# Normed tokens as two fp32r parts in place of three bf16 parts, experts chosen tile by tile, four expert tiles in the residual's memory

## The reference

```
hf = rmsnorm(x, norm_ffn_g)                      # 256 tokens, width 1024
logits = hf @ w_router + b_router                # 32 experts
top_vals, top_idx = lax.top_k(logits, 4)
gates = softmax(top_vals)
for each expert e, for the tokens that chose it:
    gu = hf @ w1[e] + b1[e]                      # 1024 x 2048, float32
    act = (clip(up) + 1) * gate * sigmoid(1.702 * gate)
    y = act @ w2[e] + b2[e]                      # 1024 x 1024, float32
x = x + sum over the chosen experts of gates * y
return rmsnorm(x, norm_final_g)
```

## Time and profile before

| | us |
|---|---|
| median of 3 runs | 1248.23 |
| the profiled execution's own time | 1249.09 |
| its span in the profile | 1247.3 |
| TensorE busy | 1172.6 |
| TensorE weight loads busy | 593.5 |
| VectorE busy | 377.3 |
| ScalarE busy | 228.9 |
| GpSimd busy | 57.7 |

### The profile page before, as it was taken

The page is one execution under the profiler, slowest core; times in us unless marked ns, Lnnn a source line. Parts: engine busy times, 40 slices in busy tenths (PEclk is TensorE's granted clock), DMA queues, the critical chain, the costliest instruction groups (busy, mean ns, idle before and its releaser), DMA issues.

```text
span 1247.3 us, 17264 instructions
## 1 busy us (share of the span) xinstructions
PE 1172.6 (94%) x7208; PEld 593.5 (48%) x7208; DVE 377.3 (30%) x677; ACT 228.9 (18%) x342; POOL 57.7 (5%) x39
## 2 busy tenths in 40 slices
PE   8999999999999999999989999999999998998996
PEld 8999888888633333333333333333333333333332
DVE  5754765656522112121111122111121111111112
ACT  5444543544510001000000010000000000000001
POOL 0950000000300000000000000000000000000000
PEclk9999999999999999999999999999999999999999
DMA  9755435947899999999999999999999999999995
GB/s 309 265 202 175 164 135 202 355 152 283 360 428 428 427 428 428 428 429 428 428 428 429 428 427 428 429 428 429 429 428 428 429 428 428 428 429 429 428 428 220
DMA packets 56212, 461.88 MB, mean 370 GB/s; under 512 B 5617, under 2 KB 7346, under 8 KB 31634
## 3 DMA queue, kind: packets, MB, share of 16 engines
q1 hardware_dynamic: 52664, 457.99, 88.6%
q10 hardware_dynamic: 3514, 3.40, 0.9%
HBM read 460.30 MB, written 1.07 MB: 370 GB/s over the span
## 4 chain that ended last, share of the span: by engine, by line
PE 57%; DMA 39%; DVE 1%; ACT 1%; issue 1%; SPq 0%; DVEq 0%; ACTq 0%
DMA w_ring<-in_w 17%; PE ps L1207 15%; DMA behind_xb<-in_w 14%; PE ps L1257 11%; DMA behind_watt<-in_w 7%; PE ps L942 3%; PE ps L943 3%; PE ps L944 3%; PE ps L1301 3%; PE ps L1185 2%; PE ps L935 2%; PE ps L938 2%; PE ps L937 2%; PE ps L954 1%; PE ps L1080 1%; PE ps L1082 1%
## 5 line engine op out<-in xcount | busy, mean ns | idle before, releaser
L1207 PE MATMUL ps<-w_ring,A_W 128*64 128x512 f32 x1232 | 278.6, 597 | 33.3 <-DMA w_ring<-in_w 33.0
L1207 PEld LDWEIGHTS ps<-w_ring,A_W 128*64 128x64 f32 x1232 | 84.4, 136 | 204.5 <-issue 142.2
L1713 DVE TENSOR_SCALAR A_W<-ps 128x512 f32<-128x512 f32 x32 | 22.1, 692 | 499.3 <-PE ps L1207 499.3
L1257 PE MATMUL ps<-w_ring,A_W 128*64 128x512 f32 x624 | 141.4, 595 | 0.0
L1380 DVE TENSOR_TENSOR w_parts<-w_ring,w_parts 128x1024 fp32r<-128x1024 f32 x76 | 105.7, 1403 | 84.2 <-ACT w_parts L654 84.2
L850 ACT ACTIVATE A_W<-A_W 128x512 f32<-128x512 f32 x32 | 20.2, 630 | 526.1 <-DVE A_W L1713 526.1
L1207 PE MATMUL ps<-A_QK,A_W 128*64 128x512 f32 x416 | 94.8, 597 | 10.9 <-DMA A_QK<-in_w 10.9
L654 ACT ACTIVATE w_parts<-w_ring 128x1024 fp32r<-128x1024 f32 x76 | 80.1, 1059 | 75.7 <-PE ps L944 37.7
L1257 PEld LDWEIGHTS ps<-w_ring,A_W 128*64 128x64 f32 x624 | 42.5, 136 | 72.1 <-issue 70.5
L854 ACT ACTIVATE A_W<-ps 128x512 f32<-128x512 f32 x32 | 19.1, 598 | 299.8 <-PE ps L1238 299.8
L942 PE MATMUL ps<-w_parts,hT_hi 128*128 128x512 f32 x176 | 69.4, 394 | 0.0
(11 more groups left out here) (246 smaller groups left out, 1285.0 us busy)
## 6 DMA issues: line engine op xcount, KB each, us to landing
w_ring<-in_w SPq DMA_DIRECT2D x115, 2048.0 KB, 43.7
A_QK<-in_w SPq DMA_DIRECT2D x38, 2048.0 KB, 42.8
behind_watt<-in_w SPq DMA_DIRECT2D x19, 2048.0 KB, 43.7
behind_xb<-in_w SPq DMA_DIRECT2D x19, 2048.0 KB, 43.7
w_ring<-in_w_in SPq DMA_DIRECT2D x36, 1024.0 KB, 7.3
w_ring<-in_w_ret_branch SPq DMA_DIRECT2D x2, 2048.0 KB, 11.8
A_W<-in_w_out SPq DMA_DIRECT2D x1, 2560.0 KB, 14.3
xb<-in_x SPq DMA_DIRECT2D x4, 512.0 KB, 3.8
```

The costliest lines, as they stand in the source:

```text
L1207: mm = pe.matmul(o, XT[:, k, :], tile[:, j, c * HALF:(c + 1) * HALF], start=(k == 0), stop=(k == KC - 1))
L1257: mm = pe.matmul(ps[CAP * c:CAP * c + CAP, 3, :], lhs, w2_tile(flat)[:, q % W2_ROWS, c * HALF:(c + 1) * HALF], start=False, stop=(q == FQ ...
```

## The change

The normed tokens become two fp32r parts: `xs_hi`, which ScalarE rounds (`high_part`), and `xs_lo`, the rest, which VectorE subtracts (`low_part`, in the place of `first_rest`). The steps of the second and third bf16 part go away on ScalarE (8 instructions) and GpSimd (4). [...] A gather is 8 x 2 x 2 = 32 matmuls in place of 48.

VectorE chooses the experts of tile 0 and tile 1 one after the other (`choose_experts`), with one half of the low parts of tile 1 between them and the other half behind the selection. TensorE starts the logits of tile 1 when half of the transposes are stored, with 8 fewer fills ahead and 20 in place of 30 behind. ScalarE copies the first gathered tokens ahead of the gates' exponentials. Four tiles of the experts (`sg`, `act_sb`, `actT`, `y_sb`) move from 2048:4096 of `A_W`, where `xs_lo` now lies, to 6144:8192, the residual's place, so their first writers wait until the residual is in PSUM (`s_res`).

```diff
+        xs_lo = nc.alloc_sbuf_tensor_at("xs_lo", [P, TT, D], F32R, offset=nc.sbuf_base - 4 * 8192 + 4 * 2048)
+        s_one = nc.alloc_sbuf_tensor_at("s_one", [P, TT, CAP], F32R, offset=nc.sbuf_base - 4 * 8192 + 4 * 5632)
-        xs = nc.alloc_sbuf_tensor_at("xs", [P, 3, TT, D], BF16, offset=nc.sbuf_base - 4 * 2304)
+        xs_hi = nc.alloc_sbuf_tensor_at("xs_hi", [P, TT, D], F32R, offset=nc.sbuf_base - 4 * 2304)
...
-            second_rest(0, 0, 0)
-            second_rest(1, 0, 1)
-            second_rest(2, 1, 0)
-            second_rest(3, 1, 1)
             pool.wait_ge(s_lo, 2 * TT)
             pool.memset(sc_w, 0.0).then_inc(main.swe, 1)
+            pool.wait_ge(s_res, TT)
             pool.memset(y_sb, 0.0).then_inc(main.ye, 1)
...
-            middle_part(0)
             root(1)
             high_part(2)
             high_part(3)
-            middle_part(1)
-            middle_part(2)
-            middle_part(3)
-            for n in range(4):
-                low_part(n)
+            act.wait_ge(main.gathered, 1)
+            act.activation(XT.rearrange("p k s -> p (k s)"), bank(2), ACT.Copy).then_inc(main.x, 1)
             act.wait_ge(s_tk, 1)
...
-            fill(1, 8)
+            pe.wait_ge(s_xte, 3)
+            logits(1, range(4))
             pe.wait_ge(s_xte, 4)
-            logits(1, range(KC)).then_inc(s_lg, 1)
-            fill(2, 30)
+            logits(1, range(4, KC)).then_inc(s_lg, 1)
+            fill(2, 20)
...
                 for k in range(KC):
-                    for part in range(3):
+                    for part in range(2):
                         for t in range(TT):
-                            mm = pe.matmul(ps[:, 2, k * CAP:(k + 1) * CAP], xs[:, part, t, k * P:(k + 1) * P],
-                                           s_one[:, t, :], start=(part == 0 and t == 0), stop=(part == 2 and t == 1))
+                            mm = pe.matmul(ps[:, 2, k * CAP:(k + 1) * CAP], (xs_hi, xs_lo)[part][:, t, k * P:(k + 1) * P],
+                                           s_one[:, t, :], start=(part == 0 and t == 0), stop=(part == 1 and t == 1))
...
+            def choose_experts(t):
                 dve.wait_ge(s_lg, t + 1)
+                link(dve.scalar_tensor_tensor(lg[t], ps[:, t, 0:N_EXP], rstd[:, t:t + 1], br_sb[:, :], ALU.mult, ALU.add))
+                link(dve.max(best[:, t, :], lg[t]))
+                link(dve.max_index(ids[:, t, :].bitcast(U32), best[:, t, :], lg[t]))
...
+            choose_experts(0)
+            low_part(2)
+            choose_experts(1)
...
             slots(main, 0, 0)
+            low_part(3)
+            dve.wait_ge(s_lo, 2 * TT)
...
             dve.wait_ge(s_used, W1_UNITS)
+            dve.wait_ge(s_res, TT)
             activate(main, 0)
```

More of the change, by code:

```diff
@@ L200, in hybrid_block_kernel @@
         xg = A_W[:, 0:2048].rearrange("p (t d) -> p t d", t=TT)
-        rest = A_W[:, 2048:4096].rearrange("p (t d) -> p t d", t=TT)
         x2 = A_W[:, 6144:8192].rearrange("p (t d) -> p t d", t=TT)
-        chosen = A_W[:, 4096:4096 + TT * TOP_K * N_EXP].rearrange("p (t j e) -> p t j e", t=TT, j=TOP_K)
+        chosen = A_W[:, 5888:5888 + TT * TOP_K * N_EXP].rearrange("p (t j e) -> p t j e", t=TT, j=TOP_K)
         weighed = A_W[:, 4352:4352 + TT * TOP_K * N_EXP].rearrange("p (t j e) -> p t j e", t=TT, j=TOP_K)
@@ L226, in hybrid_block_kernel @@
         ul = A_W[:, 1536:2048]
[L227 to L230, removed]
+        sg = A_W[:, 6144:6656]
+        act_sb = A_W[:, 6656:7168]
+        actT = A_W[:, 7168:7680]
+        y_sb = A_W[:, 7680:8192]
         bias = bias_sb[0:BIAS_ROWS, :]
@@ L795, in high_part @@
                 act.wait_ge(s_r2, t + 1)
[L796 to L806, removed]
+                act.activation(xs_hi[:, t, cols], xg[:, t, cols], ACT.Copy, scale=rstd[:, t:t + 1]).then_inc(s_hi, 1)
             def root(t):
@@ L836, in _ @@
                                accum_out=gden[:, t:t + 1]).then_inc(s_tke, 1)
-            act.wait_ge(main.gathered, 1)
-            act.activation(XT.rearrange("p k s -> p (k s)"), bank(2), ACT.Copy).then_inc(main.x, 1)
             for t in range(TT):
@@ L1191, in gather_first @@
                 pe.wait_ge(main.slots, 1)
-                for part, ready in enumerate((s_hi, s_mid, s_lo)):
+                for part, ready in enumerate((s_hi, s_lo)):
                     pe.wait_ge(ready, 2 * TT)
@@ L1195, in gather_first @@
                         for t in range(TT):
-                            mm = pe.matmul(ps[:, 2, k * CAP:(k + 1) * CAP], xs[:, part, t, k * P:(k + 1) * P],
+                            mm = pe.matmul(ps[:, 2, k * CAP:(k + 1) * CAP], (xs_hi, xs_lo)[part][:, t, k * P:(k + 1) * P],
                                            s_one[:, t, :], start=(part == 0 and k == 0 and t == 0),
-                                           stop=(part == 2 and t == 1), skip_group_check=True)
+                                           stop=(part == 1 and t == 1), skip_group_check=True)
                 mm.then_inc(main.gathered, 1)
@@ L1600, in residual_scale, with low_part @@
                 dve.wait_ge(s_r2, t + 1)
-            def first_rest(n):
+            def low_part(n):
                 t, h, cols = HALVES[n]
                 dve.wait_ge(s_hi, n + 1)
-                dve.scalar_tensor_tensor(rest[:, t, cols], xg[:, t, cols], rstd[:, t:t + 1], xs[:, 0, t, cols],
-                                         ALU.mult, ALU.subtract).then_inc(s_rest, 1)
+                dve.scalar_tensor_tensor(xs_lo[:, t, cols], xg[:, t, cols], rstd[:, t:t + 1], xs_hi[:, t, cols].bitcast(F32),
+                                         ALU.mult, ALU.subtract).then_inc(s_lo, 1)
             residual(0)
             residual_scale(0)
-            first_rest(0)
-            first_rest(1)
+            low_part(0)
+            low_part(1)
             residual(1)
@@ L1626, in _ @@
[L1626 to L1634, removed]
@@ new lines, in choose_experts @@
+                experts = expert_sb[:, :].rearrange("p (a e) -> p a e", a=1).broadcast_to([P, TOP_K, N_EXP])
+                owners = ids[:, t, 0:TOP_K].bitcast(U32).rearrange("p (j a) -> p j a", a=1).broadcast_to([P, TOP_K, N_EXP])
+                link(dve.tensor_tensor(chosen[:, t], experts, owners, ALU.is_equal))
+                dve.tensor_reduce(mask_bf[:, t, :], chosen[:, t].rearrange("p j e -> p e j"), AX.X, ALU.max).then_inc(s_mask, 1)
+            choose_experts(0)
+            low_part(2)
```

25 lines of the change are left out of this document (3 added, 22 removed).

## The result

| | before | after |
|---|---|---|
| median of the runs, us | 1247.9 (1246.42 to 1249.64, 4 runs) | 1274.99 (1272.97 to 1277.21, 4 runs) |
| ratio, 95% interval | | 1.0221 (1.0209 to 1.0233) |
| span of the profiled execution, us | 1247.3 | 1275.3 |
| mean granted clock of TensorE | 0.995 | 0.971 |

The changed kernel is 27 us slower, where the prediction's sum had 4.2 us, and lies outside the range. From the page of the changed kernel: the slices of the granted clock and of the transfer rate, the shares of the chain, and one group of matmuls. The last line is the same group on the page of the kernel before.

The account below looks back on a forecast made before the run. Transfers pace the expert stretch at 29.37 us an expert, against TensorE's 26.06. Added TensorE work of 71.4 + 1.4 + 0.3 = 73.1 us, less 68.9 us of slack, gives +4.2 us: 1252.5 us, range 1247.4 to 1257 us.

Parts of the forecast that it names:

- the prediction's sum: Whole kernel: 71.4 + 1.4 + 0.3 = 73.1 us more TensorE work, less 68.9 us of slack: +4.2 us.
- the slack between them: Expert loop: TensorE can lose 68.9 us, 2.30 us in each of 30 gathers, before the end moves.
- a gather of more than 3.75 us: Loop's gather: the forecast's own case, 1250 to 1256.5 us, chance 55%.
- +2.38 us: Loop's gather: added TensorE time for each, 3.89 in place of 1.51 us, 71.4 us over 30.
- If the clock falls again: Router stage: a low clock would meet the first gather, with loads twice as long, up to 1.7 us more.
- The gather at 3.89 us: Loop's gather: 32 fp32r matmuls at 120 ns each, 3.84 us, and about 0.05 us for the first load.
- The rival's price: Loop's gather: loads pace matmuls at 111 ns, +2.1 us each, end at 1248 to 1250 us; chance 37%.
- It decides from a gather of about 3.75 us down.: Loop's gather: at 3.75 us (117 ns a matmul) or less, the load-paced rival holds and transfers set the end.
- The router stage: Ahead of the loop: the first expert's start moves by +0.3 us, between -0.1 and +1.6 us.
- The loop's start: Ahead of the loop: the second gather, no longer hidden under the activation, puts the first matmul at 352.3 us, +1.4 us.
- The closed gap: Transfer queue: an earlier first expert closes its gap, the end comes 1.35 us earlier, 1246.9 us; chance 2%.
- What costs nothing: ScalarE, VectorE and queues: moved exponentials, gate tables, residual copies, final gain, token copy and selection add no time.

Follow-up runs that it names:

- e8: The kernel before with 192 in place of 64 columns for each of the 48 bf16 matmuls of the loop's gather: 1248.17 us, ratio 1.0004.
- e5: The kernel before with nine extra bf16 matmuls in each block of a gather, 120 in place of 48: 1264.35 us, ratio 1.0145.
- The last kernel: The changed kernel with 42 fills, block-by-block first gather, bf16 first part (64 columns) and fp32r second part (192 columns): 1246.75 us, ratio 0.9996.

## Why the prediction was wrong

What the prediction says of the bound holds: TensorE's own pace, the transfers' pace and the slack between them. The direction was right by luck: slower was to follow from a gather of more than 3.75 us, and it is 3.69. The wide bf16 gather hid 62 us of new work in that slack, and the accounting of the result closes within a microsecond with 68.9 us in it. The step that failed is the sum. It charges the gather as a duration, "+2.38 us", and lets everything behind it run as before. The text asks about the clock only in the router stage ("If the clock falls again"). In the loop a fall costs 1.65 us, and about every second gather brings one: 28.1 us with no term and no rival of its own. Without those 28.1 the sum of what was measured, 65.4 + 4.2 - 68.9, comes to 0.7 us.

Point by point:

- *The gather at 3.89 us.* It is 3.69 us. The timeline by source line has each load at 192 ns and one every 111 ns, as in the logits:

```profile
L1156 PEld LDWEIGHTS ps<-s_one,xs_hi x496: 186/192/192, 350.0 to 1217.9; 128*128 128x128 f32 x166
```

  The rival's price was right (+2.18 us; it had +2.1), and the reason that I gave for 120 ns, the nearest row of the data type, was the wrong kind of nearness. The logits' rows, with 32 columns, had the load's 111 ns, and the runs with 64, 128 and 192 columns have it too (3.69 us for 32). Why 256 columns take 120 ns, no run shows. The term was 6.0 us too high over 30 gathers.
- *"It decides from a gather of about 3.75 us down."* For the durations alone that holds: with 3.69 us and no falls the time is 1251.1 us with the late start and 1249.2 without (192 columns), and the rival said 1248 to 1250. Its case was the right one for what it counted, but it had no falls either.
- *The router stage.* The mask came 0.85 us earlier than I had it. The clock's lower level held for 10.2 us and cost far more than "up to 1.7 us": the first gather is 2.2 us above its price, and the unit behind it 2.1 us above its own, which I had not counted at all. The first unit is freed 3.1 us later than before. In the profile with 42 fills and 192 columns both are gone. Of the 3.1 us, about 2 lie within what two executions of the old program differ by (336.22 and 334.09 us). Nor does idle time alone bring this fall: between 324 and 327 us TensorE idles 2.06 us in the profile of the kernel before, 2.05 in e8's and 2.06 in e5's, and the clock falls behind it only in the first.
- *The loop's start.* 4.2 us later in place of 1.7; the second gather itself is 3.70 us.
- *The closed gap.* It could not happen with this clock, and it was never tested. The last kernel starts its experts 2.0 us ahead of 332.54 us, but two profiles of the old router program do so too. The 1.35 us are also read from the one profile in which the clock fell, and the DMA engines were busy there for 0.89 to 0.95 of the time, so not all of it is an empty queue.
- *What costs nothing.* Of the work on ScalarE, VectorE and the queues only the copy of the second gather stands in the chain behind the first one, up to the loop (0.60 us), and the sum had that. Those zeros held.

What is shown: the falls make the time, since the same loads in the same time with more columns bring none in the loop and take away 23 of the 27 us; half of the loads, or the same ones in four pieces, bring none in the profiled executions either; and idle time is not needed for one. The Trainium skill, in "TensorE: Matmul & The Clock Gate", section on HAM oscillation, ties such falls in real kernels to gaps in which TensorE idles between its matmuls. Here the trace differs: by its records TensorE is busy for all of the 3.69 us ahead of the fall and all of the 3.41 us in it, and the measurement decides. The ends of these records are modelled, so they don't say how much of the engine works. What stays open is what times the onset, and with it why it is nearly every second gather; no run shifts the gathers against each other with all else the same.

## What to carry to other kernels

Price an exchange of matmuls twice: by the interval at which they can follow each other, where a 128 x 128 fp32r load sets 111 ns and a bf16 one of 64 columns 31 ns, and by what the new stretch does to the clock of the instructions behind it, which no duration in the old trace shows. When an instruction that the change did not touch has a longer mean than before, as the scatter here (798 for 615 ns), look at the granted clock of stretches of 3 us around it, not at the page's slices. Where loads pace a stretch, more moving columns under them (up to 192 here) cost no time and can keep the clock; it is worth a try before the stretch is cut up, since each border costs too.

## What the runs showed of the hardware

- TensorE's clock fell to its lower level with the engine 100% busy, behind 3.69 us of fp32r matmuls with 64 moving columns; not with 192 columns in the same time, with 128 not in the profiled execution (others had mean clocks down to 0.991), and not behind 1.90 us of such matmuls in the profiled execution (others down to 0.992).
- The clock's state in the same program differs between executions: in the router stage of the kernel before it fell in one of three profiles, and the first expert started at 332.54 in place of 330.22 and 330.40 us.
- A loop body that grew by 72 matmuls in each of its five experts was fetched again on each pass: 85 instruction packets in place of 26, and five stops of 2.73 to 3.13 us, with the clock low behind two of them.
- Cutting a gather of 32 into four pieces between units of 64 weight columns costs 0.8 us: a piece of 8 is 1.01 us where 8 x 111 ns are 0.89, and a unit between pieces 3.58 us where one of three in a row is 3.43.
- Pairs of bf16 and fp32r matmuls in turn do not add up to their two prices: 16 and 16 take 2.87 us, where 16 x 31 and 16 x 111 ns make 2.27.
